# Start of a two-layer decoder trunk: another loading order, and two more weight tiles of each half on TensorE

## The chip, the cores and the metric

One core of a Trainium2 chip runs the kernel. The metric is the device time of one execution in microseconds (us); lower is better. The engines are TensorE (PE), VectorE (DVE), ScalarE (ACT), GpSimd (POOL) and SyncE (SP). SP and ACT each have a queue for the transfers that they issue; both issue their first at 0.7 us.

## What is computed

Two layers over 512 tokens of width 1024, in float32. Only the first norm and its modulation matter here:

```python
c_act = jax.nn.silu(c)                                   # (1, 1024)
shift, scale, gate = ada_mod(c_act, mod_mix_w[l], mod_mix_b[l], 3)   # c_act @ w + b, w is 1024 x 3072
h = rms_norm(x, norm_pre_mix[l]) * (1.0 + scale) + shift
y = dilated_mixer(h, a_w_qkv[l], a_w_o[l], cos, sin)     # begins with h @ w_qkv
...
x = x + gate * rms_norm(y, norm_post_mix[l])
```

After it come the gated convolutional FFN, shared keys and values, differential attention and a second FFN.

## The kernel before

Each engine has its own program, written out by hand; semaphores with names join them (`pe.wait_ge(*at.done(x_scaled, 1))`). An engine works strictly in the order of its program, so that what stands behind a waiting instruction waits too. Tokens and hidden columns lie in tiles of 128. Products in float32 are made of three matmuls on rounded parts (`hhi`, `hlo` by `whi`, `wlo`).

The part that concerns us is the start, up to the first value products (some 40 us), and the second half of the modulation (up to some 60 us):

- **Small inputs.** SP first issues six small transfers: `c`, four norm vectors and `kv_norm`, as rows of 128 (semaphore `vec_landed`). ACT issues six for `row_landed` (four lambda vectors, `b_subln`, and the positions spread over 128 partitions) and then seven for `table_landed` (the biases of the modulation and the convolution weights). TensorE turns these rows into columns (`turn_rows`, L735), and VectorE copies them out of PSUM (L1976): `vcol`, `bcol`, `convc`.
- **`silu(c)`** in columns is `csil` (L1982 to L1984); ACT gives the exponential (L1421), then that of the lambdas (L1423).
- **Tokens.** SP loads `x_tok` (2 MB, L457). ACT squares and sums the four token tiles (L1428), POOL makes the inverse roots (L2472, L2473; semaphore `x_scale`), ACT scales tiles 0 and 1 and VectorE tiles 2 and 3 (L1434, L2028). TensorE turns the result in 32 transposes, four for each column tile k (L816), and ACT copies each out to `z0` (L1440).
- **Modulation of the first norm.** SP loads eight tiles `mstart` of 1 MB (L484), four for each half of the hidden columns: for half 0 tile 0 and 1 hold the shift's weights (upper and lower 512 rows), tile 2 and 3 those of the scale; 4 to 7 are the same for half 1. `start_chain` on VectorE multiplies a tile's four row blocks by columns of `csil` and adds them up in `macc0` (L2039, then L2041). TensorE then sums `macc0` over the partitions by a matmul with a column of ones (`start_sums`, L606), VectorE adds the bias (L2060, L2061) and forms the gain (L2063, semaphore `m_known`). One tile, number 4, goes another way: `shift_columns` has TensorE multiply it with `csil` as a moving operand of a single column (L758).
- **h and the first value products.** With gain and shift, ACT and VectorE make `hhi` and `hlo` from `z0` (L1450, L2073, L2075; `h_ready`), and TensorE starts `values_chunk(0, 0)` (L777), then chunk 1 with the second sums in its middle (L793), then chunks 2 and 3. Ahead of and behind the first sums TensorE runs fillers (`keep_warm`, L578) whose result nobody reads, 12 each time (`WARM_SUMS`), and 8 behind chunk 1.
- **Angles.** Between `csil` and its first chain VectorE computes the rotary angles (L2000 to L2010), which ACT needs only for the sines at 42 us, and then the `near` mask (L2014, L2015).

Of the kernel before, what the change touches and what calls it, by code (L numbers as in the profile page):

```python
# [21 lines left out]
F32 = mybir.dt.float32  # L22
F32R = mybir.dt.float32r
BF16 = mybir.dt.bfloat16
I32 = mybir.dt.int32
# [4 lines left out]
P = 128  # L30
# [84 lines left out]
def yoco_trunk(nc, x, c, positions, mod_mix_w, mod_mix_b, mod_ffn_w, mod_ffn_b,  # L115
# [16 lines left out]
    WARM, WARM_START, WARM_SUMS = 24, 8, 12  # L132
# [10 lines left out]
    with ExitStack() as ctx:  # L143
# [272 lines left out]
        def tile_cols(j):  # L416
            return slice(j * P, (j + 1) * P)
# [10 lines left out]

        block = ctx.enter_context(nc.Block())
# [3 lines left out]
        def _(sp):  # L433
# [112 lines left out]
        def _(pe):  # L546
# [205 lines left out]
            def shift_columns(j):  # L752

                bank = job()
# [5 lines left out]
                job_done(ins)  # L760

            def start_sums(half):

                pe.wait_ge(*at.done(m0_summed, 2 * half + 1))
                columns_of([macc0[:, n, :] for n in range(8)])
# [53 lines left out]
            keep_warm(WARM_SUMS, ps[:, 3, :])  # L819
            pe.wait_ge(*at.done(z_out, DT - 1))  # L820
            start_sums(0)
            keep_warm(WARM_SUMS, ps[:, 3, :])
            values_chunk(0, 0)
            shift_columns(4)
# [469 lines left out]
        def _(act):  # L1294
# [112 lines left out]

            for j, v in enumerate((b_lambda_q1, b_lambda_q2, b_lambda_k1, b_lambda_k2)):
                act.dma_start(lamr[0:1, j, :], v).then_inc(*at.here(row_landed))
            act.dma_start(row1[0:1, 4, :], b_subln).then_inc(*at.here(row_landed))  # L1410
            act.dma_start(posi[:], positions.to_broadcast([P, T])).then_inc(*at.here(row_landed))
            act.dma_start(rows[0:6 * DT, 1, :], mod_mix_b.rearrange("l (r n) -> (l r) n", n=P)).then_inc(*at.here(table_landed))
# [5 lines left out]


            act.wait_ge(*at.done(t_free))  # L1420
            act.activation(EXPC, vcol[:, C_ROW:C_ROW + DT], ACT.Exp, scale=-1.0).then_inc(*at.here(c_exped))  # L1421
            act.wait_ge(*at.done(lam_summed))
            act.activation(lams[0:1, 2:4], lams[0:1, 0:2], ACT.Exp).then_inc(*at.here(lam_exped))  # L1423
            at.passed("tjob", 2)
# [16 lines left out]
            at.passed("tjob", 7)  # L1441
# [359 lines left out]
        def _(dve):  # L1801
# [190 lines left out]

            a0, a1, k0 = ang[:, 0, :], ang[:, 1, :], ang[:, 2, :]
# [18 lines left out]
            dve.wait_ge(*at.done(diffs_ready))  # L2012
            diffs = tmp[:, 3, 0:P].bitcast(I32)
            chain(dve.tensor_single_scalar(diffs, diffs, 3, ALU.bitwise_and))  # L2014
            dve.tensor_scalar(near[:, P:2 * P], diffs, 0.0, MASKED, ALU.is_gt, ALU.mult).then_inc(*at.here(near_ready))  # L2015

            bank = job_ready()
            job_read(dve.tensor_copy(small[:, NEGLAM:NEGLAM + 1], bank[:, 0:1]))
            for dst, n in ((bcol[:], NMOD), (convc[:, 0:CONV], CONV), (convc[:, CONV:2 * CONV], CONV)):
                read_columns(dst, n)  # L2020
            dve.wait_ge(*at.done(t_free, -1))
            dve.wait_ge(*at.done(t_free, -2))

            def scale_last_tokens():

                dve.wait_ge(*at.done(x_scale))
                for t in (2, 3):
                    dve.tensor_scalar(xn0[:, t, :], x_tok[:, t, :], X_RMS[:, t:t + 1], None, ALU.mult).then_inc(*at.here(x_scaled_too))  # L2028
                    at.passed("x_scaled_too")

            def start_chain(tiles, dst, number, after_two=None):

                sum_ = macc0[:, dst:dst + 4, :].rearrange("p a n -> p (a n)")
                for n, j in enumerate(tiles):
                    dve.wait_ge(*at.done(mods_landed[j]))
                    for k in range(DT // 2):
                        src, row = mstart[:, j, k, :], j % 2 * (DT // 2) + k
                        if n == 0 and k == 0:
                            ins = dve.tensor_scalar(sum_, src, csil[:, row:row + 1], None, ALU.mult)  # L2039
                        else:  # L2040
                            ins = dve.scalar_tensor_tensor(sum_, src, csil[:, row:row + 1], sum_, ALU.mult, ALU.add)  # L2041
                        if n < len(tiles) - 1 or k < DT // 2 - 1:
                            chain(ins)
                        if n == 0 and k == 1 and after_two is not None:
                            after_two()
                ins.then_inc(*at.here(m0_summed, number))

            def shift_read():

                bank = job_ready()  # L2050
                col = MIX[0] + 4
                job_read(dve.tensor_tensor(modc[:, col:col + 4], bank[:, 0:4], bcol[:, col:col + 4], ALU.add))

            def sums_read(half):

                bank = job_ready()
                col, gain = MIX[0] + 4 * half, MIX[0] + DT + 4 * half
                if half:
                    dve.wait_ge(*at.done(t_free, -1))
                dve.tensor_tensor(modc[:, col:col + 4], (modc if half else bcol)[:, col:col + 4], bank[:, 0:4], ALU.add)  # L2060
                job_read(dve.tensor_tensor(modc[:, gain:gain + 4], bank[:, 4:8], bcol[:, gain:gain + 4], ALU.add))  # L2061
                dve.wait_ge(*at.done(t_free, -1))
                dve.scalar_tensor_tensor(presc[:, 4 * half:4 * half + 4], modc[:, gain:gain + 4], 1.0,  # L2063
                                         vcol[:, PRE_MIX + 4 * half:PRE_MIX + 4 * half + 4], ALU.add, ALU.mult).then_inc(*at.here(m_known, half))

            def h_rest(k, whole):

                if not whole:
                    gain, shift = presc[:, k:k + 1], modc[:, MIX[0] + k:MIX[0] + k + 1]
                    dve.wait_ge(*at.done(m_known, k // 4))  # L2070
                    if k >= 3:
                        dve.wait_ge(*at.done(h_ready, k - 3))
                    chain(dve.tensor_scalar(tmp[:, k % 3, :], z0[:, k, :], gain, shift, ALU.mult, ALU.add))  # L2073
                dve.wait_ge(*at.done(h_hi, k))
                dve.tensor_tensor(hlo[:, k, :], tmp[:, k % 3, :], hhi[:, k, :].bitcast(F32), ALU.subtract).then_inc(*at.here(h_ready, k))  # L2075

            start_chain((0, 1), 0, 0, scale_last_tokens)
            start_chain((2, 3), 4, 1)
# [360 lines left out]
        def _(pool):  # L2439
# [27 lines left out]
            pool.wait_ge(*at.done(near_ready))  # L2467
            select(near[:].rearrange("p (b k) -> p b k", k=P), [[0, 2], [-1, P]], 0, 1, MASKED).then_inc(*at.here(masks_ready))

            def rms(dst, sums, at_):  # L2470
                dst, sums = dst[:, at_], sums[:, at_]
                chain(pool.tensor_scalar(dst, sums, NORM_EPS, None, ALU.add))  # L2472
                return pool.tensor_tensor(dst, dst, neghalf[:, at_], ALU.pow)  # L2473

# [18 lines left out]
            pool.wait_ge(*at.done(x_squared, NT - 1))  # L2493
            rms(X_RMS, X_SUM, slice(0, NT)).then_inc(*at.here(x_scale))
# [74 lines left out]
```

## Time and profile before

| | us |
|---|---|
| median of 3 runs | 1460.94 (1459.55 to 1462.33) |
| the profiled execution, its own time | 1459.9 |
| its span, from the first to the last instruction | 1458.0 |
| TensorE busy | 1407.2 (97% of the span) |
| VectorE busy | 889.1 (61%) |
| ScalarE busy | 588.7 (40%) |
| POOL busy | 146.2 (10%) |
| mean granted TensorE clock | 0.986 |

The profile comes from one execution. Busy time counts an engine as busy while an instruction runs, a filler too; a matmul that moves one column counts like one that moves 512. An entry such as "x16" is a number of records: a float32 matmul that moves one column leaves two (16 of them are 32 records).

### The profile page before, as it was taken

How to read it: one execution, taken by the hardware profiler on the slowest of the kernel's cores; microseconds unless marked ns; L12 is line 12 of the kernel's file. 1: busy time of each engine (PE TensorE's matmuls, PEld its weight loads, DVE VectorE, ACT ScalarE, POOL GpSimd, SP SyncE). 2: the span in 40 equal slices, each digit the busy share in tenths (PEclk: the TensorE clock that was granted, in tenths of full speed). 3: DMA queues.
4: the chain of work that ended last, by engine and by line, in shares of the span. 5: the costliest groups of instructions: out<-in, count | busy, mean ns of one | idle time of the engine just before them, and what ended most of it. 6: DMA issues, size and time to landing. Idle time of an engine off the chain costs nothing.

```text
span 1458.0 us, 18234 instructions
## 1 busy us (share of the span) xinstructions
PE 1407.2 (97%) x7091; PEld 1153.7 (79%) x7096; DVE 889.1 (61%) x1572; ACT 588.7 (40%) x1018; POOL 146.2 (10%) x250
## 2 busy tenths in 40 slices
PE   4999999999999999999999999998999999999998
PEld 3789888888798788887887787776888878887886
DVE  7777877674458777763556538887358444443223
ACT  4533444345443334332124526776443333332212
POOL 2001100000211111110112101221221000000000
PEclk9999999999999999999999999998999999999999
DMA  9437423331146655552661221212126333232321
GB/s 334 140 85 233 145 88 117 101 102 30 29 137 199 185 169 178 179 182 87 202 188 58 87 73 58 59 59 87 30 85 186 92 96 92 88 100 89 100 89 70
DMA packets 168667, 171.51 MB, mean 118 GB/s; under 512 B 5269, under 2 KB 140806, under 8 KB 168582
## 3 DMA queue, kind: packets, MB, share of 16 engines
q1 hardware_dynamic: 154224, 119.59, 27.2%
q0 software_dynamic: 13824, 50.34, 10.7%
q8 instruction: 57, 0.93, 0.3%
q10 hardware_dynamic: 534, 0.41, 0.1%
q14 instruction: 28, 0.23, 0.0%
HBM read 168.22 MB, written 2.10 MB: 117 GB/s over the span
## 4 chain that ended last, share of the span: by engine, by line
PE 82%; DVE 8%; ACT 4%; issue 3%; POOL 2%; DMA 1%; SPq 0%; ACTq 0%; DVEq 0%; POOLq 0%
PE ps L624 19%; PE ps L552 15%; PE ps L554 15%; PE ps L553 15%; PE ps L1087 3%; PE ps L900 2%; PE ps L793 2%; PE ps L864 2%; ACT prob L1702 2%; PE ps L606 1%; PE ps L595 1%; PE ps L1204 1%; DVE prob L2355 1%; POOL osum L2537 1%; PE ps L674 1%
## 5 line engine op out<-in xcount | busy, mean ns | idle before, releaser
L552 PE MATMUL ps<-hhi,whi 128*128 128x512 f32 (+1 forms) x1008 | 398.6, 395 | 5.2 <-DVE hlo L1890 4.6
L1815 DVE TENSOR_TENSOR wlo<-raw,whi 128x1024 fp32r<-128x1024 f32 x200 | 244.0, 1221 | 245.7 <-ACT whi L1312 245.4
L554 PE MATMUL ps<-hhi,wlo 128*128 128x512 f32 (+1 forms) x1008 | 390.5, 387 | 0.0
L553 PE MATMUL ps<-hlo,whi 128*128 128x512 f32 (+1 forms) x1008 | 390.1, 387 | 0.0
L1312 ACT ACTIVATE whi<-raw 128x1024 fp32r<-128x1024 f32 x200 | 210.1, 1052 | 257.1 <-PE ps L624 175.7
L552 PEld LDWEIGHTS ps<-hhi,whi 128*128 128x128 f32 x1008 | 191.4, 190 | 47.0 <-issue 6.4
L554 PEld LDWEIGHTS ps<-hhi,wlo 128*128 128x128 f32 x1008 | 191.4, 190 | 41.9
L553 PEld LDWEIGHTS ps<-hlo,whi 128*128 128x128 f32 x1008 | 191.7, 190 | 39.6 <-issue 1.0
L1940 DVE SCALAR_TENSOR_TENSOR macc<-mraw,csil,macc 128x256 f32<-128x256 f32 x294 | 142.2, 484 | 13.4 <-DMA mraw<-in_mod_ffn_w_dram 4.2
L624 PE MATMUL ps<-whi,ghi 128*128 128x512 f32 x352 | 110.8, 396 | 1.7 <-DVE tmp L2294 1.7
L624 PE MATMUL ps<-whi,glo 128*128 128x512 f32 x352 | 110.8, 396 | 0.0
L624 PE MATMUL ps<-wlo,ghi 128*128 128x512 f32 x352 | 110.5, 394 | 0.0
L2278 DVE SCALAR_TENSOR_TENSOR tmp<-ps,convc,tmp 128x511 f32<-128x511 f32 x88 | 65.8, 748 | 51.5 <-ACT tmp L1640 50.0
L1650 ACT ACTIVATE ghi<-tmp 128x512 fp32r<-128x512 f32 x44 | 27.8, 632 | 155.5 <-DVE tmp L2294 155.5
L1640 ACT ACTIVATE tmp<-ps,convc 128x512 f32<-128x512 f32 x44 | 34.2, 778 | 114.6 <-PE ps L554 114.5
L624 PEld LDWEIGHTS ps<-whi,ghi 128*128 128x128 f32 x352 | 65.7, 188 | 18.7 <-DVE tmp L2294 2.6
L624 PEld LDWEIGHTS ps<-wlo,ghi 128*128 128x128 f32 x352 | 66.1, 188 | 16.1
L624 PEld LDWEIGHTS ps<-whi,glo 128*128 128x128 f32 x352 | 66.1, 188 | 15.9
L2500 POOL DMA_DIRECT2D mraw<-in_mod_ffn_w_dram x48 | 36.3, 756 | 352.3 <-DVE macc L1940 279.5
L2294 DVE TENSOR_TENSOR tmp<-ps,tmp 128x512 f32<-128x512 f32 x44 | 30.4, 690 | 58.5 <-issue 45.7
L2472 POOL TENSOR_SCALAR stat<-stat 128x1 f32<-128x1 f32 (+1 forms) x29 | 8.7, 301 | 471.8 <-ACT tmp L1351 426.3
L1647 ACT ACTIVATE tmp<-tmp 128x512 f32<-128x512 f32 x44 | 27.9, 633 | 50.6 <-DVE tmp L2278 50.6
(282 smaller groups left out, 2031.1 us busy)
## 6 DMA issues: line engine op xcount, KB each, us to landing
mraw<-in_mod_ffn_w_dram POOLq DMA_DIRECT2D x48, 512.0 KB, 4.2
raw<-in_ffn_w_gate_dram SPq DMA_DIRECT2D x44, 512.0 KB, 3.8
raw<-in_ffn_w_up_dram SPq DMA_DIRECT2D x44, 512.0 KB, 3.8
raw<-in_ffn_w_down_dram SPq DMA_DIRECT2D x44, 512.0 KB, 3.6
mraw<-in_mod_mix_w_dram POOLq DMA_DIRECT2D x32, 512.0 KB, 3.9
raw<-in_a_w_qkv_dram SPq DMA_DIRECT2D x28, 512.0 KB, 4.1
mstart<-in_mod_mix_w_dram SPq DMA_DIRECT2D x8, 1024.0 KB, 14.5
mraw<-in_kv_mod_w_dram POOLq DMA_DIRECT2D x16, 512.0 KB, 3.8
```

Of the source, the lines that this page charges most:

```text
L552: pe.matmul(out_, whi[:, slot, cols], rhs_hi, start=first, stop=False)
L553: pe.matmul(out_, whi[:, slot, cols], rhs_lo, start=False, stop=False)
L554: return pe.matmul(out_, wlo[:, slot, cols], rhs_hi, start=False, stop=last)
L624: mm = pe.matmul(ps[:, 2 * t + half, :], part[:, k, tile_cols(t)], w[:, half * 512:half * 512 + 512], start=(first and n == 0), stop=(last ...
L1087: mm = pe.matmul(ps[:, V_BANKS[t], :], a[:, k, tile_cols(t)], b[:, slot, w], start=(k == 0 and n == 0), stop=(k == DT - 1 and n == 2))
L1312: act.activation(whi[:, slot, :], raw[:, slot, :], ACT.Copy).then_inc(*at.here(hi_ready, ahead))
L1640: act.activation(tmp[:, 0, :], acc[at.at("bank", 3)], ACT.Identity, bias=convc[:, base + 3 * FT + ft:base + 3 * FT + ft + 1], scale=convc[ ...
L1815: dve.tensor_tensor(wlo[:, slot, :], raw[:, slot, :], head, ALU.subtract).then_inc(*at.here(lo_ready, ahead))
L1940: ins = dve.scalar_tensor_tensor(sum_, src, factor, sum_, ALU.mult, ALU.add)
L2278: ins = dve.scalar_tensor_tensor(conv, bank[:, 0:T - shift], tap(t, ft), conv, ALU.mult, ALU.add)
L2294: dve.tensor_tensor(tmp[:, 2, :], bank, tmp[:, 1, :], ALU.mult).then_inc(*at.here(acc_free))
L2500: pool.dma_start(mraw[:, at.at("mod", 2)], src).then_inc(*at.here(m_landed))
```

## The change

Lines with `+` are the new ones; line numbers of the new program are some tens higher or lower. ACT, not SP, issues the six small transfers of `vec_landed`, ahead of its own; it issues the seven of `table_landed` only behind the two exponentials. Tiles 1 and 3, and 4 and 6, are now multiplied by TensorE with `csil` as the moving column (`start_products`), into the same bank in which `start_sums` then adds the partition sums of the other two; VectorE's chains take tiles 0, 2, 5 and 7 alone. The angles stand behind the first two chains, the `near` mask just before them, and POOL makes the inverse roots ahead of that mask. `WARM_SUMS` is 6.

```diff
-    WARM, WARM_START, WARM_SUMS = 24, 8, 12
+    WARM, WARM_START, WARM_SUMS = 24, 8, 6
...
-            sp.dma_start(rows[C_ROW:C_ROW + DT, 0, :], c[0].rearrange("(r n) -> r n", n=P)).then_inc(*at.here(vec_landed))
-            for dst, src in ((PRE_MIX, norm_pre_mix), (POST_MIX, norm_post_mix), (PRE_FFN, norm_pre_ffn), (POST_FFN, norm_post_ffn)):
-                sp.dma_start(rows[dst:dst + 2 * DT, 0, :], src.rearrange("l (r n) -> (l r) n", n=P)).then_inc(*at.here(vec_landed))
-            sp.dma_start(rows[KVN:KVN + DT, 0, :], kv_norm.rearrange("(r n) -> r n", n=P)).then_inc(*at.here(vec_landed))
             sp.dma_start(x_tok[:], x[0].rearrange("(t p) d -> p t d", p=P)).then_inc(*at.here(x_landed))
...
-            def shift_columns(j):
...
+            def start_products(half, j):
+
+                pe.wait_ge(*at.done(c_ready))
                 pe.wait_ge(*at.done(mods_landed[j]))
+                if half and j == 4:
+                    job()
                 for n in range(4):
                     for k in range(DT // 2):
-                        ins = pe.matmul(bank[:, n:n + 1], mstart[:, j, k, tile_cols(n)], csil[:, k:k + 1],
-                                        start=(k == 0), stop=(k == DT // 2 - 1))
+                        row = j % 2 * (DT // 2) + k
+                        pe.matmul(start_columns(half)[:, j // 2 % 2 * 4 + n:j // 2 % 2 * 4 + n + 1], mstart[:, j, k, tile_cols(n)], csil[:, row:row + 1],
+                                  start=(j in (1, 4) and n == 0 and k == 0), stop=False, skip_group_check=True)
+
+            def start_sums(half):
+
+                pe.wait_ge(*at.done(m0_summed, 2 * half + 1))
+                for n in range(8):
+                    ins = pe.matmul(start_columns(half)[:, n:n + 1], macc0[:, n, :], onesf[:, 0:1], start=False, stop=True, skip_group_check=True)
                 job_done(ins)
...
+            start_products(0, 1)
             pe.wait_ge(*at.done(x_scaled, 1))
             pe.wait_ge(*at.done(x_scaled_too, 1))
             for k in range(DT):
+                if k == 6:
+                    start_products(0, 3)
...
             values_chunk(0, 0)
-            shift_columns(4)
+            start_products(1, 4)
+            start_products(1, 6)
             values_chunk(0, 1, lambda: start_sums(1))
...
+            start_chain(0, 0, 0)
+            scale_last_tokens()
+            start_chain(2, 4, 1)
...
-            start_chain((0, 1), 0, 0, scale_last_tokens)
-            start_chain((2, 3), 4, 1)
             split_rest(0)
             sums_read(0)
             h_rest(0, False)
             h_rest(1, True)
             split_rest(1)
-            start_chain((5,), 0, 2)
+            start_chain(5, 0, 2)
             h_rest(2, True)
             h_rest(3, True)
-            start_chain((6, 7), 4, 3)
+            start_chain(7, 4, 3)
             split_rest(2)
-            shift_read()
             sums_read(1)
```

**TensorE's program between the small turns and the second fillers.** `xn` are the scaled tokens, `csil,mstart` the products of a modulation tile with the moving column. Before:

```order
L735 MATMUL ps<-identf,rows 128x112 [waits t_free1,table_landed]
L735 MATMUL ps<-identf,rows 128x88 [waits t_free0]
L735 MATMUL ps<-identf,rows 128x88 [waits t_free1]
L816 MATMUL ps<-identf,xn 128x128 [waits t_free1,x_scaled_too,x_scaled]
...
L578 MATMUL ps<-causal,identb 128x512 [waits masks_ready]
L578 MATMUL ps<-causal,identb 128x512 x11
L606 MATMUL ps<-onesf,macc 128x1 [waits t_free0,m0_summed,z_out]
L606 MATMUL ps<-onesf,macc 128x1 x7
L578 MATMUL ps<-causal,identb 128x512 x12
```

And now:

```order
L733 MATMUL ps<-identf,rows 128x112 [waits t_free1,table_landed]
L733 MATMUL ps<-identf,rows 128x88 [waits t_free0]
L733 MATMUL ps<-identf,rows 128x88 [waits t_free1]
L763 MATMUL ps<-csil,mstart 128x1 [waits mods_landed1,c_ready]
L763 MATMUL ps<-csil,mstart 128x1 x15
L825 MATMUL ps<-identf,xn 128x128 [waits t_free1,x_scaled_too,x_scaled]
...
L763 MATMUL ps<-csil,mstart 128x1 [waits mods_landed3,c_ready]
L763 MATMUL ps<-csil,mstart 128x1 x15
...
L576 MATMUL ps<-causal,identb 128x512 x5
L770 MATMUL ps<-onesf,macc 128x1 [waits m0_summed,z_out]
L770 MATMUL ps<-onesf,macc 128x1 x7
L576 MATMUL ps<-causal,identb 128x512 x6
```

Sixteen products stand between the turns that wait for the tables and the first transpose, and sixteen between the transposes of column tiles 5 and 6. Behind chunk 0 the row `L758` with its 16 matmuls (tile 4) has become two such rows (tiles 4 and 6).

**ScalarE's queue from its last row transfer to the squares.** Before:

```order
L1411 DMA posi<-in_positions_dram 128x512
L1412 DMA rows<-in_mod_mix_b_dram 48x128
L1413 DMA rows<-in_mod_ffn_b_dram 48x128
...
L1417 DMA rows<-in_ffn_conv_b_dram 22x128
L1421 ACT_TABLE_LOAD
L1421 ACTIVATE small<-vcol 128x8 [waits t_free0]
L1423 ACTIVATE lams<-lams 1x2 [waits lam_summed]
L1428 ACTIVATE tmp,stat<-x_tok 128x1024 [waits x_landed]
```

And now:

```order
L1425 DMA posi<-in_positions_dram 128x512
L1428 ACT_TABLE_LOAD
L1428 ACTIVATE small<-vcol 128x8 [waits t_free0]
L1430 ACTIVATE lams<-lams 1x2 [waits lam_summed]
L1432 DMA rows<-in_mod_mix_b_dram 48x128
L1433 DMA rows<-in_mod_ffn_b_dram 48x128
...
L1437 DMA rows<-in_ffn_conv_b_dram 22x128
L1441 ACTIVATE tmp,stat<-x_tok 128x1024 [waits x_landed]
```

The seven table transfers have moved from ahead of the two exponentials to between them and the squares.

**VectorE from the tables' columns to the first sums.** `macc<-mstart,csil` are the chains. Now (before, the angles, L2000 to L2010, and the mask stood ahead of the first of these rows, and each chain had eight instructions):

```order
L1989 COPY bcol<-ps 128x112 [waits t_ready]
L1989 COPY convc<-ps 128x88 [waits t_ready] x2
L2027 TENSOR_SCALAR macc<-mstart,csil 128x512 [waits mods_landed0,t_free0,t_free1]
L2029 SCALAR_TENSOR_TENSOR macc<-mstart,csil,macc 128x512 [waits v_chain] x3
L2017 TENSOR_SCALAR xn<-x_tok,stat 128x1024 [waits x_scale]
L2017 TENSOR_SCALAR xn<-x_tok,stat 128x1024
L2027 TENSOR_SCALAR macc<-mstart,csil 128x512 [waits mods_landed2]
L2029 SCALAR_TENSOR_TENSOR macc<-mstart,csil,macc 128x512 [waits v_chain] x3
L2062 TENSOR_SCALAR tmp<-tmp 128x128 [waits diffs_ready]
...
L2072 CAST ang<-posi 128x512
```

The chains and the scaling of the last two token tiles stand behind the copies of the tables' columns as before, but nothing long stands ahead of those copies.

## Rows read from the trace of the kernel before

**Rows 1.** The page: busy time, share of the span, instructions.

```profile
PE 1407.2 (97%) x7091; PEld 1153.7 (79%) x7096; DVE 889.1 (61%) x1572; ACT 588.7 (40%) x1018; POOL 146.2 (10%) x250
```

**Rows 2.** Chain that ended last, 21 to 54 us: start, duration, what.

```profile
21.26 5.16 PE ps L816 x32
26.69 2.32 PE ps L578 x10
...
31.23 3.54 PE ps L606 x16
34.77 4.22 PE ps L578 x12
38.99 5.60 PE ps L777 x24
44.59 3.46 PE ps L758 x32
48.05 4.46 PE ps L793 x12
52.51 1.68 PE ps L606 x16
```

**Rows 3.** Timeline, all engines, to 37 us: start, duration, engine, line.

```profile
2.43 0.39 ACTq L1411 DMA_DIRECT2D posi<-in_positions_dram  x1
...
3.38 0.40 SPq L457 DMA_DIRECT2D x_tok<-in_x_dram  x1
...
6.16 0.65 DVE L1972 TENSOR_TENSOR lamr<-lamr 1x128 f32<-1x128 f32 x1 [0.86 <-DMA posi<-in_positions_dram]
6.22 0.47 ACTq L1417 DMA_DIRECT2D rows<-in_ffn_conv_b_dram  x1
...
8.13 0.19 ACT L1423 ACTIVATE lams<-lams 1x2 f32<-1x2 f32 x1
...
10.04 0.43 DVE L2000 CAST ang<-posi 128x512 f32<-128x512 int32 x1
...
12.50 1.06 ACT L1428 ACTIVATE tmp<-x_tok 128x1024 f32<-128x1024 f32 x1 [4.19 <-DMA x_tok<-in_x_dram]
...
12.97 0.45 PE L735 MATMUL ps<-identf,rows 112*128 112x112 f32 x1 [2.39 <-DMA rows<-in_ffn_conv_b_dram]
...
16.84 0.26 DVE L1976 COPY bcol<-ps 128x112 f32<-128x112 f32 x1
...
17.89 0.49 DVE L2039 TENSOR_SCALAR macc<-mstart,csil 128x512 f32<-128x512 f32 x1
...
20.53 4.68 DVE L2041 SCALAR_TENSOR_TENSOR macc<-mstart,csil,macc 128x512 f32<-128x512 f32 x6
...
36.19 0.69 DVE L2075 TENSOR_TENSOR hlo<-tmp,hhi 128x512 fp32r<-128x512 f32 x1 [0.37 <-ACT hhi L1450]
```

**Rows 4.** TensorE by stretch: from:to, length, busy (records), clock, DMA share, GB/s.

```profile
21.26:24.30 3.04, 3.04 (x15) 1.00 1.05 386
24.30:26.42 2.12, 2.12 (x20) 1.00 1.05 387
31.20:34.77 3.57, 3.54 (x17) 0.50 1.04 386
44.40:47.90 3.50, 3.50 (x33) 1.00 0.05 14
47.90:51.60 3.70, 3.70 (x11) 0.54 0.00 0
```

**Rows 5.** DMA queues, 6 to 7 us (q1 is SP's, q10 is ACT's): packets, MB.

```profile
q1 hardware_dynamic: 78, 0.32, 93.6%
q10 hardware_dynamic: 1, 0.00, 0.1%
```

**Rows 6.** DMA queues, 8.2 to 12.6 us.

```profile
q10 hardware_dynamic: 252, 0.10, 8.2%
```

**Rows 7.** TensorE's waits from 60 to 160 us: us in total, times, longest.

```profile
PE ps L552 <- ACT vA L1457: 0.6, 1, 0.6
```

More of the change, by code:

```diff
@@ L1991, in _, with scale_last_tokens @@
             chain(dve.tensor_scalar(small[:, SUBG:SUBG + 1], small[:, SUBLN:SUBLN + 1], 1.0 - LAM_INIT, None, ALU.mult))
+            bank = job_ready()
+            job_read(dve.tensor_copy(small[:, NEGLAM:NEGLAM + 1], bank[:, 0:1]))
+            for dst, n in ((bcol[:], NMOD), (convc[:, 0:CONV], CONV), (convc[:, CONV:2 * CONV], CONV)):
+                read_columns(dst, n)
+            dve.wait_ge(*at.done(t_free, -1))
+            dve.wait_ge(*at.done(t_free, -2))
+            def scale_last_tokens():
+                dve.wait_ge(*at.done(x_scale))
+                for t in (2, 3):
+                    dve.tensor_scalar(xn0[:, t, :], x_tok[:, t, :], X_RMS[:, t:t + 1], None, ALU.mult).then_inc(*at.here(x_scaled_too))
+                    at.passed("x_scaled_too")
@@ new lines, in start_chain @@
+            def start_chain(j, dst, number):
+                sum_ = macc0[:, dst:dst + 4, :].rearrange("p a n -> p (a n)")
+                dve.wait_ge(*at.done(mods_landed[j]))
+                for k in range(DT // 2):
+                    src, row = mstart[:, j, k, :], j % 2 * (DT // 2) + k
+                    if k == 0:
+                        ins = dve.tensor_scalar(sum_, src, csil[:, row:row + 1], None, ALU.mult)
+                    else:
+                        ins = dve.scalar_tensor_tensor(sum_, src, csil[:, row:row + 1], sum_, ALU.mult, ALU.add)
+                    if k < DT // 2 - 1:
+                        chain(ins)
+                ins.then_inc(*at.here(m0_summed, number))
@@ new lines, in sums_read @@
+            def sums_read(half):
+                bank = job_ready()
+                if not half:
+                    bank = ps[:, 3, :]
+                col, gain = MIX[0] + 4 * half, MIX[0] + DT + 4 * half
+                dve.tensor_tensor(modc[:, col:col + 4], bcol[:, col:col + 4], bank[:, 0:4], ALU.add)
+                job_read(dve.tensor_tensor(modc[:, gain:gain + 4], bank[:, 4:8], bcol[:, gain:gain + 4], ALU.add))
+                dve.wait_ge(*at.done(t_free, -1))
+                dve.scalar_tensor_tensor(presc[:, 4 * half:4 * half + 4], modc[:, gain:gain + 4], 1.0,
+                                         vcol[:, PRE_MIX + 4 * half:PRE_MIX + 4 * half + 4], ALU.add, ALU.mult).then_inc(*at.here(m_known, half))
@@ new lines, in h_rest @@
+            def h_rest(k, whole):
+                if not whole:
+                    gain, shift = presc[:, k:k + 1], modc[:, MIX[0] + k:MIX[0] + k + 1]
+                    dve.wait_ge(*at.done(m_known, k // 4))
+                    if k >= 3:
+                        dve.wait_ge(*at.done(h_ready, k - 3))
+                    chain(dve.tensor_scalar(tmp[:, k % 3, :], z0[:, k, :], gain, shift, ALU.mult, ALU.add))
+                dve.wait_ge(*at.done(h_hi, k))
+                dve.tensor_tensor(hlo[:, k, :], tmp[:, k % 3, :], hhi[:, k, :].bitcast(F32), ALU.subtract).then_inc(*at.here(h_ready, k))
@@ L1993, in _ @@
+            start_chain(0, 0, 0)
+            scale_last_tokens()
+            start_chain(2, 4, 1)
+            dve.wait_ge(*at.done(diffs_ready))
+            diffs = tmp[:, 3, 0:P].bitcast(I32)
+            chain(dve.tensor_single_scalar(diffs, diffs, 3, ALU.bitwise_and))
+            dve.tensor_scalar(near[:, P:2 * P], diffs, 0.0, MASKED, ALU.is_gt, ALU.mult).then_inc(*at.here(near_ready))
             a0, a1, k0 = ang[:, 0, :], ang[:, 1, :], ang[:, 2, :]
@@ L2010, in _ @@
             dve.tensor_scalar(ang[:, 0:2, :], ang[:, 0:2, :], limit, -limit, ALU.min, ALU.max).then_inc(*at.here(angles_ready))
[L2012 to L2075, printed above, removed]
@@ L2473, in rms @@
                 return pool.tensor_tensor(dst, dst, neghalf[:, at_], ALU.pow)
+            pool.wait_ge(*at.done(x_squared, NT - 1))
+            rms(X_RMS, X_SUM, slice(0, NT)).then_inc(*at.here(x_scale))
+            pool.wait_ge(*at.done(near_ready))
+            select(near[:].rearrange("p (b k) -> p b k", k=P), [[0, 2], [-1, P]], 0, 1, MASKED).then_inc(*at.here(masks_ready))
             def token_stage(norms):
```

31 lines of the change are left out of this document (16 added, 15 removed).

## The prediction

> **What bounds the kernel now.** I read the page first. TensorE is busy 97% of the span [rows 1], so a change that leaves its work alone can gain only where it idles, and added work on it costs its full length unless it falls into an idle stretch. Then the chain that ended last, for the start [rows 2]. TensorE's transposes begin at 21.26. The first sums (the row of 3.54 at 31.23) begin 2.2 behind the last filler before them, because VectorE's chains end only then. Twelve more fillers end at 38.99, where the first real product starts. From 38.99 the chain stays on TensorE without a gap: chunk 0 (5.60), tile 4 with a moving column (3.46), half of chunk 1 (4.46), the second sums (1.68). I call 38.99 the chunk start. From 60 to 160 us TensorE's longest wait is 0.6 [rows 7]: what it loses earlier it hardly gets back, what it gains it keeps.
>
> Third, the timeline [rows 3], for what holds the start of the transposes: the squares wait for `x_tok` (issued 3.38, first square 12.50), and 8.76 later the transposes begin. The tables have landed at 12.97, and nobody needs them before VectorE's copy at 16.84, because the angles (from 10.04) lie in front. Last, TensorE's stretches [rows 4]: two of them were granted half the clock (1.2 instead of 2.4 GHz), from 31.2 to the fillers and from 47.9 to 51.6. Ahead of the first TensorE had idled, ahead of the second it had run for 3.5 us nothing but matmuls with one moving column. The first 15 transposes took 0.20 each, the next 20 0.11, although the column says 1.00 for both: until about 24.3 TensorE ran at the slow rate.
>
> **The change, part by part.** The times are those at which things happen in the new program, against the trace before.
>
> *The positions land, R.* ACT's queue reached `posi` at 2.43 [rows 3]; it now has six more transfers ahead, for which SP needed from 0.7 to 3.38, so `posi` is issued at about 5.1. It took 3.7 to land (first user 6.16). A later transfer of the same queue, issued at 6.22 when `x_tok` was under way, had landed only at 12.97, 6.75 later [rows 3]. Between 6 and 7 us ACT's queue moved a single packet [rows 5], then 252 in 4.4 us [rows 6]. Since `x_tok` is now issued at 0.7, nearly all small transfers meet it. Bounds for R: 5.1 + 3.7 = 8.8 and 5.1 + 6.75 = 11.8.
>
> *The tables land, L.* Everything on VectorE that leads to `csil` and to the lambdas stands behind the row transfers. The second exponential ended 2.16 behind the lambdas' product at 6.16; I count 1.5, an estimate, because ACT came to it only behind its last issue (6.22 + 0.47) and a load of its function table, and both are past by now [rows 3]. Behind it ACT issues seven transfers, 3.4 until the last is begun (2.8 to 6.22), and this one lands 3.7 to 6.75 later. L is R + 8.6 to R + 11.65: 17.4 to 23.5. Neither end is nearer by a row, so I take the middle, 20.4. Before it was 12.97 at no cost; the angles that covered it are gone from there, so this lateness is new and it is on the path: TensorE's turns, `bcol`, and all behind them on both engines wait for it.
>
> *The squares* stand behind the same issues: R + 1.5 + 3.8. With R at 10.3 that is 15.6 where it was 12.50, although `x_tok` itself lands 2.6 earlier; the transposes could start 8.76 later, at 24.4. POOL's mask, now behind the roots, no longer delays them (0.4 at most).
>
> *Start of the transposes, X.* In TensorE's order stand now the turns (some 1.5, from the turn's 0.45 and the 1.05 from the copy at 16.84 to 17.89 [rows 3]), then 32 records of tile 1. At full clock 32 such records take 3.46 [rows 2]; at half clock 16 took 3.54, so 32 take 7.1 [rows 2, 4]. TensorE has done next to nothing before, and its first transposes in the old trace ran at the slow rate, so 7.1. X = 20.4 + 1.5 + 7.1 = 29.0, against 21.26; the squares' way (24.4) is hidden. VectorE's part is hidden too: chain 0 (0.49 + 3 x 0.78 = 2.8) and two token tiles end near 26, and then it has a chain (2.8) and the mask and angles (10.04 to 16.84, 6.8) until about 36, while TensorE can't be at the sums before 39 (below) [rows 3].
>
> *From X to the chunk start.* Transposes 5.2 [rows 2]; tile 3 between them 3.5 (full) to 7.1 (half); six fillers 1.4 (10 took 2.32) to 2.1 (12 took 4.22); sums 1.7 (the row at 52.51) to 3.5; then six fillers 2.1, in which h also becomes ready (the first `hlo` ended at 36.88, 2.1 behind the sums' end at 34.77) [rows 2, 3]. All at full clock that is 13.9, all at half with slow transposes (32 x 0.20 = 6.5) 22. I take 15.8: one of these stretches, the sums, at half, since a run of moving columns stands shortly ahead. Removed against before: the wait of 2.2 and twelve fillers. Chunk start 29.0 + 15.8 = 44.8, which is 5.8 later than 38.99.
>
> *Behind chunk 0.* 32 more records of moving columns (tile 6). TensorE is never idle here, so they cost their whole length: 3.5 to 7.1. After the 32 that stood there before, the granted clock was at half at once, from 47.9 on [rows 4]; so I take 6. VectorE's chains lose four instructions (3.1), but TensorE didn't wait for it in this stretch, so nothing is gained. The half-clock stretch behind (12 products in 4.46) stays.
>
> *Sum.* 5.8 + 6.0, less 0.6 for the one later wait that a late TensorE may absorb [rows 7]: 11.2. The profiled execution took 1459.9, so 1471.1; the median shown is 1.0 above it: 1472.
>
> **Two rules against these rows.** One packet of ACT's queue against 78 of SP's in the same microsecond is what makes L late. The Trainium skill (DMA: Bandwidth & Descriptors, Issuing engines are not separate DMA queues) says that transfers of different engines interleave on the same 16 DMA engines and that issuing from several only saves issue time. By it nothing holds the small ones, which is the first rival below; in the rows from 8.2 on they do interleave, at 6 to 7 us they don't.
>
> The transposes went from 0.20 to 0.11 each while TensorE ran transposes alone. The Trainium skill (TensorE: Matmul & The Clock Gate, the part on transposes) says that a transpose doesn't count as activity that releases the clock. By it all 32 would take 6.5 and the sum would be 1.3 more; the trace disagrees.
>
> **Rivals.**
> - *The small loads aren't held.* L is 17.4, its lower bound; the rest as above. For it: `posi` landed in 3.7 before. Against it: the 6.75 of the last table. X 26.0, chunk start 41.8, +2.8 + 6 - 0.6 = +8.2: 1469.
> - *The clock stays full.* The products keep TensorE occupied and no stretch falls to half. For it: it no longer idles ahead of the sums. Against it: the slow first transposes, and the fall at 47.9 after 3.5 us of just such matmuls. X = 20.4 + 1.5 + 3.5 = 25.4, chunk start 39.3 (+0.3), tile 6 +3.5, and the 12 products in 4.46 would take 2.8 (-1.7): +2.1, 1463. At R's lower bound, where the squares set X (14.1 + 8.76 = 22.9), -0.4.
> - *The tokens set the pace, and it gets faster.* If ACT is through with the tables when `x_tok` lands (0.7 + 9.1 = 9.8), X is 18.6, the chunk start 32.5 (-6.5), and with 3.5 for tile 6 the sum is -3.0: 1458 as a median. Its place is ACT's queue ahead of the squares; the point is R: it must be below 4.5, while 8.8 is my bound. Each us of R beyond costs one.
> - *Half clock everywhere.* L at 23.5, X 32.1, 22 to the chunk start, 7.1: above +20, 1481 and more. For it: three separate runs of moving columns. Against it: real products start between them.
>
> **How the numbers follow.** Forecast 0.45 (1470 to 1479), small loads not held 0.20, full clock 0.20, tokens set the pace 0.08, half clock everywhere 0.07. I predict 1472, the likeliest. A measurement of this kernel can tell about 0.2% (2.9 us) from no change: half of the full-clock case lies inside it. Slower 0.45 + 0.20 + 0.10 + 0.07 = 0.82, same 0.10, faster 0.08. The range 1462 to 1479 leaves out the fastest case, the slowest and a part of the full-clock case.
>
> **What would show it.** Right: the first square after 14; the turn of 112 rows after 17, waiting for a table; tile 1's 32 records in about 7 and the first transpose waiting for nothing but them; the chunk start near 45; 64 records of moving columns in 9 to 10 behind chunk 0, then products of 0.43; afterwards the same kernel shifted. Wrong: the turn at 14 or earlier, or VectorE's copy of `bcol` waiting for TensorE rather than for a transfer; moving columns at 0.11 a record throughout; or a stretch beyond 60 us whose length changes by more than 1, which I exclude since TensorE's order there is the same.

## The result, and the profile after

The changed kernel takes 1475.2 us (median of 4 runs, 1474.4 to 1478.3) against 1460.6 before (4 runs); the ratio is 1.0109, its interval 1.0097 to 1.0121. It is slower, by 14.6 us by the medians and by 15.9 by the ratio (14.2 to 17.7 by its interval), in the direction forecast, 3 us beyond the predicted 1472 and inside the range of 1462 to 1479.

The chain that ended last, in the profile of the changed kernel (start, duration, what), answers [rows 2]:

```profile
5.12 7.10 DMA posi<-in_positions_dram
...
15.58 6.17 DMA rows<-in_ffn_conv_b_dram
...
21.80 0.46 PE ps L733
...
23.02 6.69 PE ps L763 x32
29.71 4.30 PE ps L825 x24
34.01 4.39 PE ps L763 x32
38.40 1.81 PE ps L825 x8
40.21 2.56 PE ps L576 x6
42.77 1.94 PE ps L770 x16
...
44.73 0.16 DVE modc L2040
...
46.12 0.70 DVE hlo L2055
...
46.95 5.83 PE ps L783 x24
52.79 9.66 PE ps L763 x64
62.45 5.06 PE ps L799 x12
67.51 1.68 PE ps L770 x16
...
73.83 5.60 PE ps L783 x24
```

The start now runs over two transfers on ACT's queue: `posi` until 12.22, the last table until 21.75. Behind them TensorE is the chain, but for 2.2 us from 44.71 to 46.95, in which VectorE and ACT make the gain and the first `h` behind the first sums. In the kernel before, the last pieces ahead of the transposes were these:

```profile
15.77 0.69 DVE ang L2010
...
17.07 0.41 POOL near L2448
...
17.56 0.23 POOL stat L2472
...
19.02 2.20 ACT xn L1434 x2
```

They are the angles, the mask that POOL makes from VectorE's, and only then the inverse roots. The tokens' squares had ended at 17.20, so that the two paths were 0.4 us apart. The chunk start has gone from 38.99 to 46.95 (+8.0), and chunk 2 from 58.85 to 73.83 (+15.0; in the kernel before its 24 products begin at 58.85 behind the fillers). Little more is lost later: the span grew by 15.4.

The timeline of the changed kernel (start, duration, engine, line) shows who waited for the two transfers:

```profile
12.25 0.28 DVE L1985 TENSOR_TENSOR lamr<-lamr 1x128 f32<-1x128 f32 x1 [6.95 <-DMA posi<-in_positions_dram]
...
13.03 0.32 ACTq L1432 DMA_DIRECT2D rows<-in_mod_mix_b_dram  x1
...
16.00 1.06 ACT L1441 ACTIVATE tmp<-x_tok 128x1024 f32<-128x1024 f32 x1 [2.68 <-issue]
...
22.28 0.28 DVE L1989 COPY bcol<-ps 128x112 f32<-128x112 f32 x1 [5.85 <-PE ps L733]
...
44.73 0.16 DVE L2040 TENSOR_TENSOR modc<-bcol,ps 128x4 f32<-128x4 f32 x1 [6.56 <-PE ps L770]
```

The first table is issued only at 13.03, the first square comes at 16.00 where it was 12.50 [rows 3], and VectorE idles 5.9 ahead of its chains and 6.6 ahead of the first sums' result: its relief went into waiting. The DMA queues of the changed kernel from 2 to 5 us, with one row only because ACT's queue (q10) moved nothing at all (compare [rows 5, 6]):

```profile
q1 hardware_dynamic: 231, 0.95, 87.3%
```

The same from 12 to 16 us, though the tables were issued from 13.03 on:

```profile
q1 hardware_dynamic: 803, 1.60, 105.0%
```

Between 5 and 12 us ACT's queue did move packets in every microsecond, 21 to 60 of them, those of the smaller transfers first and those of `posi` behind them.

TensorE by stretch in the changed kernel (from:to, length, busy and records, granted clock, DMA share, GB/s):

```profile
33.80:38.30 4.50, 4.50 (x35) 0.78 0.52 172
...
52.70:62.40 9.70, 9.70 (x66) 0.71 0.20 58
62.40:67.50 5.10, 5.10 (x16) 0.54 0.00 0
```

The second stretch is tiles 4 and 6: it begins at full clock and ends at half (1.2 GHz), and the half clock goes on over half of chunk 1. Before, the same place had 0.54 over 3.7 us [rows 4]. From 38.4 to 42.8, over the last eight transposes and six fillers, the granted clock was 0.50 as well.

### The profile page after: what moved, and what is told of

It reads as the page before. It is cut to its first block, busy times and chain, and to the rows that moved or that the text cites. A ratio compares the mean times of both kernels' runs of the same rounds, so it can differ in the third digit from the quotient of the medians.

```text
span 1473.4 us, 18392 instructions
## 1 busy us (share of the span) xinstructions
PE 1421.7 (96%) x7180; PEld 1170.1 (79%) x7180; DVE 879.8 (60%) x1559; ACT 589.2 (40%) x1018; POOL 146.5 (10%) x250
## 4 chain that ended last, share of the span: by engine, by line
PE 82%; DVE 8%; ACT 4%; issue 2%; POOL 2%; DMA 1%; ACTq 0%; DVEq 0%
PE ps L622 19%; PE ps L550 15%; PE ps L552 14%; PE ps L551 14%; PE ps L1097 3%; PE ps L910 2%; PE ps L799 2%; PE ps L874 2%; ACT prob L1715 2%; PE ps L763 1%; PE ps L593 1%; PE ps L1214 1%; PE ps L604 1%; DVE prob L2359 1%; POOL osum L2542 1%
## 5 line engine op out<-in xcount | busy, mean ns | idle before, releaser
L622 PEld LDWEIGHTS ps<-wlo,ghi 128*128 128x128 f32 x352 | 66.1, 188 | 15.8
## 6 DMA issues: line engine op xcount, KB each, us to landing
mstart<-in_mod_mix_w_dram SPq DMA_DIRECT2D x8, 1024.0 KB, 15.4
```

The lines of the kernel that those rows point to most:

```text
L622: mm = pe.matmul(ps[:, 2 * t + half, :], part[:, k, tile_cols(t)], w[:, half * 512:half * 512 + 512], start=(first and n == 0), stop=(last ...
```

## The experiments

Every kernel was compared with the kernel before on its own chip; its median there lay between 1459.3 and 1460.7. So I compare ratios, and for the start the time at which chunk 2's 24 products begin in the trace (58.85 before, 73.83 changed). That time comes from a single execution. Run 8 has the same instructions as the kernel before up to chunk 0, and its execution began chunk 0 at 37.54, not at 38.99, because its first sums took 1.92 at full clock instead of 3.54 at half. So a difference of 1.5 us between two traces shows nothing by itself.

**1. The old loads in the changed kernel.** All six vector transfers are SP's again, ahead of `x_tok`, and the two exponentials stand behind the seven tables; two lines of it:

```diff
+            sp.dma_start(rows[C_ROW:C_ROW + DT, 0, :], c[0].rearrange("(r n) -> r n", n=P)).then_inc(*at.here(vec_landed))
...
             sp.dma_start(x_tok[:], x[0].rearrange("(t p) d -> p t d", p=P)).then_inc(*at.here(x_landed))
...
-            act.dma_start(rows[C_ROW:C_ROW + DT, 0, :], c_rows).then_inc(*at.here(vec_landed))
...
             act.dma_start(posi[:], positions.to_broadcast([P, T])).then_inc(*at.here(row_landed))
-
-            act.wait_ge(*at.done(t_free))
-            act.activation(EXPC, vcol[:, C_ROW:C_ROW + DT], ACT.Exp, scale=-1.0).then_inc(*at.here(c_exped))
```

> The changed kernel with the loading order of before (SP issues the six vector transfers ahead of the tokens, ScalarE issues the tables ahead of its exponentials); all else as changed. Theory (late small loads are the first part of the loss): the tables land near 13 again and the squares start at 12.5, but tile 1 lands only near 18, its products take 7 at half clock, the transposes start near 25 instead of 29.7, and the chunk start moves from 46.95 to about 42: some 4.7 us less than the changed kernel, about 1470.5. Rival (only the added work on TensorE costs): within 1 of the changed kernel, about 1475.

Ratio 1.0090 (1.0075 to 1.0104), median 1473.1. The chain of this kernel:

```profile
17.92 6.96 PE ps L767 x32
...
41.95 5.85 PE ps L787 x24
47.79 9.85 PE ps L767 x64
...
68.85 5.60 PE ps L787 x24
```

In the trace the theory holds: the chunk starts at 41.95 as expected (42), chunk 2 comes 5.0 earlier than in the changed kernel. By the ratios only 2.8 of it arrive, and the two intervals overlap. Between chunk 2 and some 390 us this execution took 2.3 more than the one of the changed kernel, with the same instructions there; it had three stretches of half clock there as the other did, but one of them was twice as long (0.66 over 10 us from 360 on, against 0.66 over 5 from 367 on). The expected 1470.5 was missed by 2.6. The products of tile 1 take 6.96 here and 6.69 with the new loads; they cost the front here because they begin only when their tile has landed, at 17.9. A clearer price of the loads is runs 3 and 7, which differ in the loads alone: 1.0068 and 1.0031, some 5.4 us, with intervals that don't touch (71.14 and 66.21 for chunk 2).

**2. The new loads alone, in the kernel before.** The six vector transfers go to ScalarE's queue ahead of its own, the tables behind the exponentials; the first lines of it:

```diff
-            sp.dma_start(rows[C_ROW:C_ROW + DT, 0, :], c[0].rearrange("(r n) -> r n", n=P)).then_inc(*at.here(vec_landed))
...
+            act.dma_start(rows[C_ROW:C_ROW + DT, 0, :], c_rows).then_inc(*at.here(vec_landed))
```

> The kernel before with nothing but the new loading order on SP and ScalarE. Theory: positions land near 12, tables near 22, VectorE's first chain starts near 23.3 instead of 17.9, the whole start shifts by about 5.4, TensorE behind 39 us is unchanged: about 1466. Rival (the angles on VectorE and the fillers cover late loads): within 1.5 of before, about 1461.

Ratio 1.0042 (1.0030 to 1.0054), median 1465.7: 6.1 slower, chunk 2 at 64.60 (+5.75). The chain names the same transfer:

```profile
5.15 7.21 DMA posi<-in_positions_dram
...
44.75 5.60 PE ps L775 x24
```

The whole start is the old one, shifted by 5.7. Angles and fillers cover nothing of the late positions, since everything on VectorE stands behind them. They do cover the late tables: the turn of 112 rows began at 21.93, when they had landed, and VectorE came to the copy at 22.55 without having waited.

**3. The second half's work as before, in the changed kernel.**

```diff
-            start_products(1, 6)
...
-            start_chain(7, 4, 3)
+            start_chain(6, 4, None)
+            start_chain(7, 4, 3, True)
```

> The changed kernel, but TensorE multiplies only tile 4 in the second half; VectorE's chains take 5, and 6 with 7, as before. Theory (tile 6 costs its whole length, most of it at half clock): the 9.7 us of moving columns behind chunk 0 become 3.5, the half-clock stretch behind shrinks, about 6.5 less than the changed kernel: 1468.7. Rival (VectorE's chains are then the bound, so that its relief was worth something): 1472 or more.

Ratio 1.0068 (1.0053 to 1.0083), median 1468.9, as the theory had it: 6 less than the changed kernel. VectorE has its four instructions back, and no loss by it shows. The profiled execution took 1471.9 (all of them 1466.5 to 1472.3) and began chunk 2 only 2.7 earlier, at 71.14: chunk 0 took 6.56 and the 32 records 4.46, both partly at half clock:

```profile
34.00:51.00 17.00, 16.78 (x78) 0.60 0.37 127
```

**4. Tiles 4 and 6 apart.** Tile 4 now stands in chunk 0, behind the twelve products of its first step (three for each token tile):

```diff
                             for n, (a, b) in enumerate(((hhi, whi), (hhi, wlo), (hlo, whi))):
                                 mm = pe.matmul(ps[:, t, 0:value_cols(g)], a[:, k, tile_cols(t)], b[:, slot, w], start=(k == 0 and n == 0), stop=False)
+                        if c == 0 and k == 0:
+                            start_products(1, 4)
...
-            start_products(1, 4)
             start_products(1, 6)
```

> The changed kernel with the products of tile 4 moved into the middle of chunk 0, so that 12 real products stand between them and those of tile 6. Theory A (half clock follows only from a run longer than one tile): both runs at full clock, 7.0 instead of 9.7, and less half clock behind, about 1472. Theory B (one tile's run of 3.5 us is enough, as before at 47.9): each run is followed by its own half-clock stretch over real products, which costs as much as it saves: 1474 to 1477.

Ratio 1.0107 (1.0091 to 1.0122), median 1475.3: no gain, as theory B had it.

```profile
52.47 3.46 PE ps L763 x32
55.93 2.91 PE ps L783 x12
58.84 4.48 PE ps L763 x32
63.32 5.04 PE ps L801 x12
```

The first run stays at full clock here and the second falls to half inside and behind itself. The two together take 7.9 instead of 9.7, but the half clock behind stays, and this execution began chunk 0 later by 1.6 and chunk 2 by 0.9 (74.69).

**5. Tile 3 alone, where TensorE would idle.**

```diff
-            keep_warm(WARM_SUMS, ps[:, 3, :])
+            scale_products(3)
             pe.wait_ge(*at.done(z_out, DT - 1))
             start_sums(0)
-            keep_warm(WARM_SUMS, ps[:, 3, :])
+            keep_warm(WARM_SUMS // 2, ps[:, 2, :])
...
-            start_chain((2, 3), 4, 1)
+            start_chain((2,), 4, 1)
```

> The kernel before with tile 3 alone multiplied by TensorE, behind its transposes where the first fillers stood (they fall away), the six second fillers instead of twelve, loads, angles and second half as before. Theory (moving columns are worth it only where TensorE would idle and VectorE's chains are what is waited for): the chains end near 28 instead of 31.1, the products end near 30, the chunk starts between 34 and 37 instead of 38.99: 2 to 4 less than before, about 1456.5. Rival (such products always cost more than they save, through half clock): the same as before or slower, 1459 to 1462.

Ratio 0.9999 (0.9984 to 1.0015): the rival. The runs lie between 1455.4 and 1465.1 (12 of them; 31 of the kernel before on this chip between 1455.5 and 1463.6). In the profiled one, the slowest (1465.1), the chain reads

```profile
27.64 3.99 PE ps L759 x32
31.63 3.41 PE ps L779 x16
...
37.63 7.03 PE ps L792 x24
```

The chunk starts 1.4 earlier, and 1.4 more go into chunk 0, which took 7.03 instead of 5.60. The stretch from 30 to 41 us was granted 0.53. Chunk 2 began at 60.50. The faster executions left no trace, so how they ran the start is open.

**6. Six fillers instead of twelve in the kernel before** (`WARM_SUMS = 6`).

> The kernel before with 6 fillers instead of 12 ahead of and behind the first sums. Theory (behind the sums h is ready 2.1 later, so that six fillers at half clock fill just this): the chunk starts near 37 instead of 39, but its first products run at half clock until the clock rises; between 0 and 2 less than before. Rival (the fillers are what lifts the clock): the half-clock stretch lasts longer over real products, 1 to 3 more than before.

Ratio 0.9992 (0.9976 to 1.0008), not to be told from no change, although in its trace chunk 2 began at 54.46, 4.4 earlier than in the one of before: 1.6 of this is first sums at full clock (1.94), 1.5 the first half of chunk 1 at full clock. Its profiled execution shows that the fall of the clock behind a run of moving columns is not certain. These are its 32 records of tile 4 and what follows:

```profile
41.50:45.00 3.50, 3.50 (x34) 1.00 0.70 248
45.00:48.00 3.00, 3.00 (x14) 1.00 0.00 0
```

Full clock behind the very same 3.5 us that were followed by half clock in [rows 4].

**7. The front alone**: old loads and the old second half in the changed kernel (edits 1 and 3 together).

> The changed kernel with the old loading order and the second half as before: what is left of the change is tiles 1 and 3 on TensorE, the angles behind the chains and the shorter fillers. Theory (parts add up: loads 5.75 by the second run, front products 3, tile 6 about 7): the chunk starts near 42, the second half takes as long as before, 3 more than before: 1462.5. Rival (with the loads back the front gains): below 1459.5.

Ratio 1.0031 (1.0018 to 1.0043), median 1463.3: 4.5 slower, 1.5 more than the theory's 3. Three parts of the change are still together in it: the products of tiles 1 and 3, the later angles and the shorter fillers. In the kernel before, the fillers (run 6) and angles with fillers (run 9) were worth nothing that could be told from no change, so that the products are the likely cause; no run had them alone. The profiled execution (1467.1, all 1460.6 to 1467.8) began chunk 2 at 66.21, 7.4 later than before.

**8. Tile 6 alone**, in the kernel before, where tile 4 already was on TensorE.

```diff
-            shift_columns(4)
+            start_products(4)
+            start_products(6)
...
-            start_chain((6, 7), 4, 3)
-            shift_read()
+            start_chain((7,), 4, 3)
```

> The kernel before with tile 6 on TensorE behind tile 4 and one chain less on VectorE; nothing else. Theory: the chunk starts at 39 as before; 32 more records at half clock, 6 to 7 more than before: 1466. Rival (moving columns cost 3.5 for a tile wherever they stand): 3.5 more, 1463.

Ratio 1.0040 (1.0027 to 1.0054), median 1465.1: 5.9 slower; the rival's 3.5 is 0.24% and outside the interval. Chunk 2 began at 64.23 (+5.4, with a chunk start 1.5 earlier).

```profile
37.54 5.60 PE ps L784 x24
43.14 9.95 PE ps L761 x64
```

**9 and 10. Angles out of the way, with old loads**, in the kernel before; with six fillers (run 9) and with twelve (run 10). The angles' first five instructions go behind the first split, the rest behind `shift_read`, and ScalarE's sines behind two value chunks:

```diff
             split_rest(0)
...
+            chain(dve.tensor_copy(k0, posi[:]))
...
+            chain(dve.scalar_tensor_tensor(a0, k0, -part1, a0, ALU.mult, ALU.add))
             sums_read(0)
...
             shift_read()
+            for part in (part2, part3):
+                chain(dve.scalar_tensor_tensor(a0, k0, -part, a0, ALU.mult, ALU.add))
```

> The kernel before with six fillers instead of twelve on either side of the first sums and with the angles taken out of the way of the first chain: their first five instructions stand between the first rest of weights and the first sums, the others ahead of the second sums, where VectorE waited 2.6 and 3.4; ScalarE makes the sines behind the second half's h. Loads and products as before. Theory (in the kernel before it is the angles, not the tables, that hold the first chain at 17.9): the chain starts near 15.3 with tile 0, ends near 28.5 instead of 31.1, the chunk starts near 34.5 to 36: 3 to 4 less than before, 1456. Rival (the transposes or tile 3's landing are next in line): under 1 less.

> The same with the twelve fillers of before. Theory: the chains end 2.6 earlier, the fillers keep their length, 2 to 2.6 less than before, 1457. Rival: the same as before, because half clock takes the gain.

Ratios 1.0004 (0.9991 to 1.0017) and 0.9991 (0.9982 to 1.0001). The 3 to 4 expected of run 9 didn't come; the 2 to 2.6 expected of run 10 (0.9982 to 0.9986) stand at the edge of its interval, so that neither they nor no change can be excluded. In the traces chunk 2 began at 59.16 and 56.76; of the 2.1 that run 10 gains there 1.6 is first sums that took 1.92 at full clock, as they did in run 8. VectorE's timeline in run 10 shows what held the chains:

```profile
15.25 0.49 DVE L2021 TENSOR_SCALAR macc<-mstart,csil 128x512 f32<-128x512 f32 x1 [0.88 <-DMA mstart<-in_mod_mix_w_dram]
15.78 0.75 DVE L2023 SCALAR_TENSOR_TENSOR macc<-mstart,csil,macc 128x512 f32<-128x512 f32 x1
18.66 1.42 DVE L2010 TENSOR_SCALAR xn<-x_tok,stat 128x1024 f32<-128x1024 f32 x2 [2.13 <-POOL stat L2475]
...
30.50 1.22 DVE L1816 TENSOR_TENSOR wlo<-raw,whi 128x1024 fp32r<-128x1024 f32 x1
```

The chain does start at 15.25, 2.6 earlier, but the scaling of the last two tokens stands behind its second instruction and waits 2.1 for the inverse roots. The chains end at 30.5 instead of 31.0. The angles were only the first of the things in the way.

**11. The angles back in front, in the changed kernel.**

> The changed kernel with the angles back in their old place, ahead of the tables' copies. Theory (VectorE waits 5.9 for the tables there and idles 6.6 ahead of the first sums, so the angles' place is worth nothing with the new loads): within 1.5 of the changed kernel, 1474 to 1476. Rival (the angles behind the chains delay the rest of the weights and the sums): 2 or more less than the changed kernel.

Ratio 1.0122 (1.0101 to 1.0142), which overlaps the changed kernel's; median 1477.6, above what I expected, with runs from 1475.3 to 1483.3. Chunk 2 began at 73.01 in its trace, 0.8 earlier than in the changed kernel. The rival's gain of 2 or more is excluded: with late tables the angles' place gives nothing.

**12. Run 10's kernel, with four instructions of the first chain instead of two ahead of the scaling of the last tokens.**

```diff
-                        if n == 0 and k == 1 and after_two is not None:
+                        if n == 0 and k == 3 and after_two is not None:
```

> The kernel before with the angles out of the way (as in the run before the last), twelve fillers, and VectorE's four instructions of tile 0, not two, ahead of the scaling of the last two token tiles, where the run with two had it wait 2.1 for the inverse roots. Theory (behind the angles it is this wait, that is the tokens' squares, that holds VectorE's chains): the chains end near 29.0 instead of 30.5, the first sums and the chunk start move by as much, 2 to 2.5 less than before: 1457.3. Rival (the place of the half-clock stretches decides about such small shifts): within 1 of before.

Ratio 0.9975 (0.9963 to 0.9988), median 1457.3 against 1460.7 on its chip: 3.6 faster than before, and the lowest ratio here. Its interval overlaps that of run 10 (0.9982 to 1.0001), so that it is shown to be faster than the kernel before, but not than run 10.

```profile
19.04 1.42 DVE L2010 TENSOR_SCALAR xn<-x_tok,stat 128x1024 f32<-128x1024 f32 x2 [1.01 <-POOL stat L2475]
...
29.30 1.22 DVE L1816 TENSOR_TENSOR wlo<-raw,whi 128x1024 fp32r<-128x1024 f32 x1
```

The wait has shrunk to 1.0, the chains end 1.2 earlier than in run 10, and chunk 2 begins at 55.40. What holds the start now is the moved angles themselves; the chain that ended last runs over them:

```profile
30.52 0.35 DVE ang L2069
...
32.34 0.70 DVE ang L2073
...
33.06 0.16 DVE modc L2042
```

The first sums ended at 31.41, but VectorE reads them only at 33.06, behind these five instructions, and TensorE waits 1.3 for the first `h`. Run 9 is the same (angles from 31.84, the read at 34.38).

## Why the prediction was right, and where it was off

**Direction and mechanism held, the sizes were too small.** The two losses are those of the sum. In the trace the chunk start came 8.0 later, where the sum has 5.8, and 7.0 more went by until chunk 2, where it has 6.0. Apart from each other, loads alone cost 6.1 (run 2), the front's products with its shorter fillers and later angles 4.5 (run 7), tile 6 5.9 (run 8): 16.5 together, each known to within 2 us, against 15.9 (14.2 to 17.7) for the whole.

**Positions land, R: off.** My bounds were 8.8 and 11.8; `posi` was issued at 5.12, as worked out, and landed at 12.22, above both. I took the 6.75 of a small late transfer as the worst, and the larger positions took 7.1. That ACT's queue would stand still at first while SP's moves was right; the time that this costs was too small in the sum (5.2 at the middle of my bounds).

**Tables land, L: 21.75 for 20.4.** The error of R went through (1.9 from my middle of 10.3). The second exponential ended 1.1 behind R, I had 1.5; the last issue began 2.3 behind that, I had 3.4; and the last table took 6.17, near my upper bound, where I took the middle of 5.2. Together 12.22 + 1.1 + 2.3 + 6.17. The squares started at 16.00 for my 15.6 and were hidden, as said. One reason given was wrong: that the late tables hurt because the angles no longer cover them. With late positions and the angles in front VectorE comes to the tables' copy at 22.55 (run 2) and 22.33 (run 11), behind the chains it comes there at 22.28. It is the positions that delay all of VectorE's work, wherever the angles stand.

**X: 29.7 for 29.0.** The 32 records took 6.7 to 7.0, about twice the 3.46 of full clock, in every variant that had them here; 7.1 was predicted, and the full-clock rival (3.5) is refuted there. The Trainium skill (TensorE: Matmul & The Clock Gate, Part 1) has the array throttled by default until activity releases it; the durations of these records agree, though the clock column shows 1.00.

**X to the chunk start: 17.2 for 15.8.** The transposes took 6.1 instead of 5.2, tile 3's products 4.4 instead of the 3.5 that I put in, and the six fillers 2.6 instead of 1.4. Half clock fell on the end of tile 3's products (inside the stretch with 0.78), the last transposes and the fillers (0.50), and hardly on the sums (1.9), where I had put it. The size was off by 1.4; that one such stretch would cost something was right, its place was not.

**Tile 6: 6.2 for 6.** 64 records took 9.66, against 3.46 for 32. What I left out is that the half clock behind them lasts longer: chunk 1's first half took 5.06 instead of 4.46. Chunk 0, ahead of them, took 5.83 instead of 5.60. I also booked 0.6 that a later wait would give back, and it didn't: that wait of 0.6 is still there in the changed kernel, and the span grew by 0.4 more than chunk 2's delay.

**The relief of VectorE was worth nothing**, as said: it waited 6.6 for the first sums, and no loss showed when run 3 gave it back the four instructions of tile 6. Nor was the angles' new place worth anything (run 11).

**The first rival** (small loads aren't held) is refuted by the queue rows and by R and L. The Trainium skill (DMA: Bandwidth & Descriptors, Issuing engines are not separate DMA queues) says that transfers of several engines interleave. From 2 to 5 us and from 13 to 16 these did not; later they do: these are the queues of the changed kernel from 17 to 21 us.

```profile
q1 hardware_dynamic: 667, 1.30, 93.1%
q10 hardware_dynamic: 359, 0.14, 13.6%
```

**What I read wrongly in the kernel before.** I took the tokens' squares for what held its first transposes. Its chain ran over the angles and the mask on VectorE and POOL, and the squares had ended 0.4 before the inverse roots began. The sum doesn't use it.

**What stays open.** Why ACT's queue stands still for some microseconds and then moves beside SP's isn't shown by any run here. Whether TensorE's clock falls behind 3.5 us of moving columns differs between executions (it did before, it didn't in run 6), and I couldn't tell what decides; nor is it shown that the moving columns cause the fall. That this, and the place of later half-clock stretches, is what spreads the runs of one kernel by up to 10 us, and what took half of run 1's gain, is argued from the traces' stretches and not shown by a run of its own.

## What to carry to other kernels

Before small loads are moved behind or beside large ones, find who waits for them: here a 256 KB transfer, which all of VectorE's work stood behind, landed 6 us later, and it cost that much with the work that could have covered the tables still in its place (run 2). Multiplying by a matmul with one moving column costs its full length where TensorE is the bound, and here up to twice that; even where TensorE would have idled it gained nothing (run 5). If an engine's relief is the aim, look at what it waits for next: the angles moved alone brought the end of the chains 0.5 us forward of the 2.6, and with the wait behind them shortened too the kernel was clearly faster than before (0.9975). And one trace is one execution: chunk 2 began 4.4 us earlier in run 6's, and its times can't be told from those of the kernel before.

## What the runs showed of the hardware

- Transfers that ACT issues while SP's queue moves large ones can stand still for microseconds before they move beside them: no packet from 2 to 5 us, and none from 13.03, when the tables were first issued, to 16, with SP's queue at 231 packets from 2 to 5 and 803 from 12 to 16. `posi` needed 7.1 instead of 3.7, and the same again in runs 2, 3, 4 and 11 (7.0 to 7.2). The last table needed 6.2, but 6.75 with the old loads.
- Float32 matmuls with one moving column leave two records of 0.108 each at full clock (32 in 3.46), and of 0.22 at half (16 in 3.54 at a granted 0.50). Tile 1's 32 at the start took 6.7 to 7.0, 0.21 to 0.22 each.
- They did not keep the clock up: in all profiles here but that of run 6, half clock began within such a run of products behind or in chunk 0, or up to 1.5 us behind it (run 12). The clock also falls where none stand near: in the kernel before it was 0.52 from 403 to 406.5 us, and in the 8 us ahead TensorE had no such matmul.
